# Differential attention: a tile's four turns set one by one between single projection products, on one Trainium2 core

## What is computed

```python
def diff_attention(q, k, v, lam, lambda_init, subln_g, rel_bias):
    ...
        logits = jnp.einsum('bqhmd,bkhmd->bhmqk', qb, k).astype(jnp.float32) * scale + bias
        p = jax.nn.softmax(logits, axis=-1)
        attn = (p[:, :, 0] - lam * p[:, :, 1]).astype(v.dtype)
        return jnp.einsum('bhqk,bkhe->bqhe', attn, v)
    ...
    o = rms_norm(o, subln_g) * (1.0 - lambda_init)
    return o.reshape(b, s, W_A)
...
    h = rms_norm(x, pre_g)
    u = h @ w_in
...
    ya = ya * jax.nn.silu(ag)
```

## Time and profile before

| | |
|---|---|
| median of three executions | 1346.05 us |
| the profiled execution | 1346.24 us |
| its span, first to last instruction | 1344.3 us |
| TensorE matmuls | 1323.4 us busy, 98% of the span |
| TensorE weight loads | 1079.8 us, beside the matmuls |
| VectorE, ScalarE, GpSimd | 45%, 41%, 22% |
| DMA | 53 GB/s over the span |
| branch A's tiles | 65 to 307 us, by the first and last turn of line 920 |

### The profile page before, as it was taken

The page is one execution under the profiler, slowest core; times in us unless marked ns, Lnnn a source line. Parts: engine busy times, 40 slices in busy tenths (PEclk is TensorE's granted clock), DMA queues, the critical chain, the costliest instruction groups (busy, mean ns, idle before and its releaser), DMA issues.

```text
span 1344.3 us, 17653 instructions
## 1 busy us (share of the span) xinstructions
PE 1323.4 (98%) x6671; PEld 1079.8 (80%) x6671; DVE 602.1 (45%) x1166; ACT 551.1 (41%) x1075; POOL 302.3 (22%) x199
## 2 busy tenths in 40 slices
PE   8999999999999999999999999999999999999998
PEld 5778887888888778788888888888877887888887
DVE  6454555556100487786321335455544115435222
ACT  5355455553111477777311135555553113223210
POOL 4112212222322321130222312221211223213100
PEclk9999999999999999999999999999999999999999
DMA  5211112111111110000111211111101113322111
GB/s 181 77 41 41 40 41 56 52 32 51 48 48 47 47 32 6 28 17 24 35 57 42 78 47 48 47 49 46 32 24 32 47 47 147 137 81 80 66 40 39
DMA packets 25694, 71.61 MB, mean 53 GB/s; under 512 B 2921, under 2 KB 4841, under 8 KB 25490
## 3 DMA queue, kind: packets, MB, share of 16 engines
q1 hardware_dynamic: 25618, 70.57, 16.7%
HBM read 66.34 MB, written 4.23 MB: 52 GB/s over the span
## 4 chain that ended last, share of the span: by engine, by line
PE 93%; DVE 3%; ACT 2%; issue 1%; POOL 0%; ACTq 0%; DVEq 0%
PE ps L846 18%; PE ps L865 14%; PE ps L1202 13%; PE ps L1243 10%; PE ps L1400 7%; PE ps L1420 6%; PE ps L1087 6%; PE ps L885 2%; PE ps L1024 2%; PE ps L940 2%; PE ps L1172 2%; PE ps L1426 2%; PE ps L1055 1%; PE ps L1146 1%; PE ps L1122 1%; PE ps L873 1%
## 5 line engine op out<-in xcount | busy, mean ns | idle before, releaser
L669 POOL TENSOR_TENSOR w_lo<-stage,w_hi 128x1024 fp32r<-128x1024 f32 (+1 forms) x92 | 195.7, 2127 | 660.0 <-ACT w_hi L1470 660.0
L1470 ACT CAST w_hi<-stage 128x1024 fp32r<-128x1024 f32 (+1 forms) x92 | 86.2, 937 | 280.3 <-PE ps L846 198.8
L1982 DVE TENSOR_TENSOR pt_lo<-ps,pt_hi 128x512 fp32r<-128x512 f32 (+2 forms) x160 | 97.1, 607 | 80.6 <-ACT pt_hi L1800 40.3
L865 PE MATMUL ps<-h_hi,w_hi 128*128 128x512 f32 x272 | 110.3, 405 | 0.0
L846 PE MATMUL ps<-h_hi,w_hi 128*128 128x512 f32 x352 | 108.7, 390 | 0.0
L846 PE MATMUL ps<-h_lo,w_hi 128*128 128x512 f32 x352 | 108.5, 389 | 0.0
L846 PE MATMUL ps<-h_hi,w_lo 128*128 128x512 f32 x352 | 108.4, 389 | 0.0
L1202 PE MATMUL ps<-h_hi,w_hi 128*128 128x512 f32 x256 | 106.8, 417 | 0.0
L865 PE MATMUL ps<-h_hi,w_lo 128*128 128x512 f32 x272 | 106.2, 391 | 0.0
L865 PE MATMUL ps<-h_lo,w_hi 128*128 128x512 f32 x272 | 106.1, 390 | 0.0
L1202 PE MATMUL ps<-h_hi,w_lo 128*128 128x512 f32 x256 | 100.4, 392 | 0.0
(11 more groups left out here) (297 smaller groups left out, 2902.8 us busy)
## 6 DMA issues: line engine op xcount, KB each, us to landing
stage<-in_w_gates SPq DMA_DIRECT2D x24, 512.0 KB, 3.5
stage<-in_w_qkvg_a SPq DMA_DIRECT2D x19, 512.0 KB, 6.1
stage<-in_w_qkvg_c SPq DMA_DIRECT2D x16, 512.0 KB, 3.5
stage<-in_w_branch SPq DMA_DIRECT2D x24, 256.0 KB, 2.7
m<-in_x_tok SPq DMA_DIRECT2D x8, 512.0 KB, 7.9
y<-in_x_tok SPq DMA_DIRECT2D x8, 512.0 KB, 3.6
stage<-in_w_pg SPq DMA_DIRECT2D x16, 256.0 KB, 3.1
out<-y SPq DMA_DIRECT2D x16, 256.0 KB, 2.0
```

The source lines that it names most:

```text
L669: nc.gpsimd.tensor_tensor(dst, stage[:, staged, 0:width], f32(hi), ALU.subtract).then_inc(w_ready, 1)
L865: done = mm(ps[:, half_bank(T), :], w[:, slot, k * P:(k + 1) * P], h[:, k, g * SEQ:(g + 1) * SEQ], start=k == 0 and part == 0, stop=k == K ...
L1470: nc.scalar.copy(dst, stage[:, staged, 0:width]).then_inc(w_hi_done, 1)
L1982: sub = lambda out, whole, hi: nc.vector.tensor_tensor(out, whole, f32(hi), ALU.subtract)
```

## The change

The early part of a half is counted in products, no longer in chunks: `TURN_AT = 6` in place of 3 chunks (9 products). `turn_a` now sets one product of the half ahead of its second, third and fourth turn. The 15 products behind are as before. At T = -2 and T = -1, which have no `turn_a`, the three products follow `between`. What `turn_values`, `sum_squares` and `spread_rstd` do stays as it was, ahead of the first turn of `turn_a`, and so now stands behind 6 products and no longer behind 9.

```diff
-EARLY_CHUNKS = 3
+TURN_AT = 6
...
-            def project_half(T, chunks):
+            def project_half(T, first, end):
...
-                for k in chunks:
-                    for part, (w, h) in enumerate([(w_hi, h_hi), (w_hi, h_lo), (w_lo, h_hi)]):
-                        done = mm(ps[:, half_bank(T), :], w[:, slot, k * P:(k + 1) * P],
-                                  h[:, k, g * SEQ:(g + 1) * SEQ],
-                                  start=k == 0 and part == 0, stop=k == KC - 1 and part == 2)
+                for n in range(first, end):
+                    k, part = divmod(n, 3)
+                    w, h = [(w_hi, h_hi), (w_hi, h_lo), (w_lo, h_hi)][part]
+                    done = mm(ps[:, half_bank(T), :], w[:, slot, k * P:(k + 1) * P], h[:, k, g * SEQ:(g + 1) * SEQ],
+                              start=n == 0, stop=n == 3 * KC - 1)
                 return done
...
                 for k in range(QT):
+                    if k:
+                        project_half(T, TURN_AT + k - 1, TURN_AT + k)
                     done = nc.tensor.transpose(ps[:, 0, k * P:(k + 1) * P], s[:, T % 2, 0, k * P:(k + 1) * P],
                                                ident[:, :])
                 done.then_inc(p_turned, 1)
...
-                project_half(T, range(EARLY_CHUNKS))
+                project_half(T, 0, TURN_AT)
                 between(T)
-                project_half(T, range(EARLY_CHUNKS, KC)).then_inc(half_done, 1)
+                if T < 0:
+                    project_half(T, TURN_AT, TURN_AT + QT - 1)
+                project_half(T, TURN_AT + QT - 1, 3 * KC).then_inc(half_done, 1)
```

## The result

The changed kernel takes 1348.95 us (median of 20 executions), the kernel before 1346.05 us (median of 20). The ratio is 1.0021, 95% interval 1.0015 to 1.0027: slower, by 2.9 us. Forecast were 1349.0 us and a range of 1346.5 to 1351.2.

The account below looks back on a forecast made before the run. TensorE was taken as the bound, with a matmul under way for 98% of the span. Borders +1.1 and late copy +1.8 made +2.9 us, so 1349.0 us against the median 1346.05; range 1346.5 to 1351.2.

Parts of the forecast that it names:

- part 2: Values' turns, wanted 0.68 us sooner, wait for ScalarE's copy at tiles 1, 7, 15 and 23: +1.8 us.
- part 1: On TensorE in branch A, four single turns replace each run, paying its borders 96 more times: +1.1 us.
- Nothing else pays: No work added, `p_turned` no sooner, other engines' work unmoved, stages behind branch A only shifted by some 3 us.
- The copy was late: Answers the second rival: ScalarE's values' copy comes soon enough, only borders remain, 1347.2 us; chance 0.18.
- third rival: At TensorE's single turns, every change of kind costs more and held-up turns cannot load ahead: 1350.5 us; chance 0.17.
- One sign: In the profile after, the product behind a single turn starts 0.11 after it; under 0.1 favours the first rival.
- first rival: On TensorE, a single turn hides its cost, taking 0.06, saving 4.8 us: 1343.0 us; chance 0.10.
- The rule on weight loads: The skill's 107 ns per load would start held-up turns 0.05 later at four places, 0.2 us more; forecast used 0.06.

Follow-up runs that it names:

- the scores at the turns: Kernel before, with the score pair of 15 even tiles moved to just ahead of the tile's turns; 1344.6 us, ratio 0.9991 to the kernel before.
- e5_pairs: Changed kernel, with the turns as two pairs behind 8 products, one product between; 1346.24 us, ratio 1.0002 to the kernel before.
- e2_values_early: Changed kernel, with the tile's own four turns a run behind 9 products, values' turns still behind 6; 1348.27 us, ratio 1.0018 to before.
- e7_values_at_3: Changed kernel, with values' turns, squares and spread behind 3 products, the tile's run behind 9; 1351.99 us, ratio 1.0045 to before.

## Why the prediction was right

*The early turns meet a late copy* (part 2, +1.8 us): right in place, chain and size. Four tiles wait, 1, 7, 15 and 23; 9, 17 and 25 do not. It was 0.46 at tiles 7, 15 and 23 against 0.48, 0.35 at tile 1 against 0.38, and 2.91 - 1.16 = 1.75 in all against 1.8. Without the stall (values three products later, or the copy ahead of the scale) that part goes, and the two ways agree to 0.01 us. Twice the distance brought the longer waits and the three new ones.

*Four borders for one* (part 1, +1.1 us): right, 1.16. The choice of 0.012 within 0 to 0.02 leaned on rows rounded to 0.01, so the agreement to a tenth is luck. The average hides something: read by the distance from one tile's last turn to the next's, the single turns cost 0.05 in most even tiles and 0.02 in most odd ones. From the first to the last turn of a tile it is the same everywhere, 0.008 to 0.013 for each additional single turn, so the difference lies in the products behind the turns. What makes it was not tried.

*Nothing else pays*: right. `p_turned`, the other engines and the stages behind moved with TensorE; the rest of the program took 1037.50 us against 1037.63.

*The rivals.* A single turn did not hide its cost: the next product's load starts with the turn, and 0.35 from turn to turn is 0.01 more than the two alone, not 0.05 less. The copy was late. A change of kind did not cost more than the run's borders had shown; 0.35 is also under the 0.37 that would have spoken for the third rival. (That rival's sum takes 2.6 for turns that cannot be loaded ahead, where part 2 has 4 x 0.68 = 2.7; it decides nothing.)

*One sign could not be read as it was put.* The product behind a single turn was to start 0.11 after it, and under 0.1 was to speak for the first rival. In the PE rows it starts 0.03 after it (110.11 and 110.14). But it does so in the kernel before too: the last of four turns that start at 110.23, 0.109 apart, stands at 110.56, and the product behind it at 110.58. So the start of such a row says nothing of the turn's cost. The 0.11 stands in the load rows alone (behind tile 6's last turn, the product's load at 111.15 and the next at 111.26), and what decides against the rival is the distance from turn to turn.

*The rule on weight loads.* The turn held up at tile 7 came 0.06 behind its load, as in the earlier trace rows: four loads, 0.42 in all. By the 107 ns, an estimate, of the Trainium skill, page "TensorE: Matmul & The Clock Gate", section "LDWEIGHTS (loading the stationary operand)", it would have been 0.11. The trace does not agree: a turn's load is the shorter one here, and 0.05 of the 0.08 a tile that the scores at the turns gain is read from that.

## What to carry to other kernels

When a run of small operations is spread out, look at both its ends: if its first moves and its last does not, every input wanted at the first has lost that distance, while everything released by the last gains nothing. Count the slack of each such input at the operation that uses it, in units of the engine that is the bound, before asking what the spread itself brings. Here the turn could have started 0.20 us sooner (116.15 against 115.95) and 0.68 were taken; with 0.23 taken (`e5_pairs`) 0.01 was lost at most. The 0.09 between the copy's end and the load is less than the slack, since that load starts 0.23 ahead of its turn. And where, as in these rows, a matmul's load starts with the matmul ahead and no sooner, short operations between long ones hide nothing: a product's load (0.11) lies open behind a turn. More borders cost here (1.16 us for 93 single turns), and fewer gained.

## What the runs showed that I had not expected

Behind a border, products do not fall back to their plain distance at once: in the trace the four to nine distances behind the opened load are up to 0.236, the later ones 0.227. The 24 products behind tile 6's turns take 5.48 in the earlier trace rows, those ahead of the squares in tile 5 take 5.44 (there 12 products of `mix_a` stand between the turns and the piece, and the wide distances fall on them), and in the experiments such a piece lies between 5.44 and 5.50. Up to 0.06 us in a piece, as much as several borders, thus hangs on something other than the number of products; what sets it was not tried.

In both kernels that tried it (`e2_values_early`, `e7_values_at_3`), matmuls of 2 columns were better followed by turns than by products: 0.07 us at each such place, several times a turn's border.
